# V of all head pairs computed ahead of the attention loop and kept in DRAM

## The chip, the core and the metric

The kernel runs on one core of one Trainium2 chip. The metric is the device time of one execution in microseconds (us). Engines: PE is TensorE (matrix products), DVE is VectorE, ACT is ScalarE, POOL is GpSimd, and SP issues all the DMAs spoken of here.

## The reference, cut to what matters

One layer of an encoder: neighbourhood attention, a layer norm, a squared-ReLU MLP with a gated embedding, a second layer norm. Only the attention's projections bear on the change.

```python
def neighborhood_attention(x, w_qkv, rpb, w_o):        # x (1, 1024, 1024), w_qkv (1024, 3072)
    qkv = (x @ w_qkv).reshape(bsz, rows, GRID_W, 3, NA_HEADS, HEAD_DIM)   # 16 rows, 64 wide, 16 heads of 64
    q = qkv[:, :, :, 0] * HEAD_DIM ** -0.5
    k = qkv[:, :, :, 1]
    v = qkv[:, :, :, 2]
    def row_block(r):                                  # 8 key rows, 16 key columns around each query
        s = jnp.einsum('bqhd,bakhd->bhqak', q_r, k_b, preferred_element_type=jnp.float32)
        s = jnp.where(col_in[:, None, :], s + bias, -jnp.inf)
        pr = jax.nn.softmax(s, axis=(-2, -1))
        return jnp.einsum('bhqak,bakhd->bqhd', pr.astype(v.dtype), v_b)
    ...
    return jnp.moveaxis(out, 0, 1).reshape(bsz, seq, D_MODEL) @ w_o
```

## The kernel before

**Numbers in two parts.** Each float32 operand of a projection is split into a high and a low part (ACT copies the high part, DVE or POOL subtracts for the low part), and a product is three passes: high by high, low by high, high by low. So one projection group (a bank of 128 x 512 outputs, 8 chunks of the inner dimension) is 24 products, `GROUP_MMS`.

**The first stage** (from L1386). x is loaded in eight column chunks, turned on PE, split, and kept as `act_T_hi` and `act_T_lo`. While the chunks come in, PE fills six banks: V, K and Q of head pair 0, two halves of the tokens each (`first_products`, L1265). V comes out with channels on the partitions, so DVE copies it to `v_T` (L1058), PE turns it by four 128 x 128 transposes per half (L1281), and ACT and DVE split the turned tile (L867, L1076) into `v_hi_lo`.

**The loop over head pairs** (`pairs_loop`: pairs 0 to 5 in a hardware loop, 6 and 7 apart). Each engine has its own queue with its own order, written out by steps s = 0 to 20 or 21. A pair has 16 score units (2 heads x 8 groups of 128 queries). On PE, step s holds a slice of the next pair's projections (`project`, L1227: 144 products over 20 steps, 7.2 each), the scores of unit s (L1310), the transposes of unit s-3's probabilities (L1289) and the products with V whose tiles are ready (L1333). Pair 7 has no next pair: PE then fills its steps with 96 embedding products (L1371) and the first output products.

The other queues run beside it. In step s of pairs 0 to 6:

- DVE: normalise unit s-2 (L1110, L1112), low part of turned tile s-4 (L1084), an output sum at s = 11, 13, 19, 21 (L1119), add the bias to the scores of unit s and take the negated maximum (L1103), then an evacuation of a projection group if one is due.
- ACT: high part of turned tile s-4 (L878), the half of an output sum (L894), an evacuation of a group (L841), exp of unit s (L887), which waits for the negated maximum of s, then a weight split if one is due (L833).
- POOL: the low halves of the weight splits (L778), and the two bias tables of the next pair (L785, L787).
- SP: weights of the pair after next, bias rows (16 DMAs per head), K's copies to the other half of the partitions (`k_twice`), the attention output.

In pair 7 the order on DVE is another: the bias add comes first in its step, ahead of normalise and low part.

`EVAC_STEP` gives the steps at which a group is evacuated: V at 3 and 6 (DVE) with its transposes at 4 and 7, K at 10 and 14, Q at 17 and 20. The splits of the weights on ACT are at steps 1, 9 and 18. These lines set the order on ACT and DVE for the pairs that the change touches:

```python
                    if PARTS <= s < UNITS + PARTS:
                        turned_tile(j, s - PARTS)
                    for h, b in out_evac_at(s):
                        out_sum(j, h, b)
...
                    if more and s < UNITS:
                        add_bias(j, s)
...
                    if more and s in EVAC_STEP[2:]:
                        evac(1 - par, j + 1, EVAC_STEP.index(s))
```

`add_bias(u)` waits for unit u's scores and for the exp of u-2; PE's scores of u wait for the bias add of u-2, its transposes of u for normalise of u, its V products of tile u for the low part of u. After pair 7 come the output projection, the layer norm and the MLP (from some 440 us on); the change leaves them alone.

Of the kernel before, what the change touches and what calls it, by code (L numbers as in the profile page):

```python
# [48 lines left out]
V_, K_, Q_ = range(3)  # L49
W_COLUMN = {V_: 2 * D, K_: D, Q_: 0}  # L50
# [73 lines left out]
def build_program(nc, x, p, w_qkv, rpb, w_o, ln1_g, ln1_b, w_ff1, w_ff2, ln2_g, ln2_b, w_gate, w_proj, mask, out):  # L124
    with ExitStack() as ctx:
# [15 lines left out]

        S.rpb_rows = nc.dram_tensor("rpb_rows", [GC, HEADS, DR, 3 * GC], F32).ap()
# [29 lines left out]
        with ExitStack() as first:  # L172

            S.w = [first.enter_context(nc.sbuf_tensor(f"w_qkv_{n}", [P, 2, KC, P], F32R)) for n in ("hi", "lo")]
            S.w_hi, S.w_lo = (first.enter_context(nc.semaphore(f"w_{n}_done")) for n in ("hi", "lo"))
            attention(nc, S, x, w_qkv, rpb, mask, w_o, p, w_proj, ln1_g, ln1_b, w_gate)
# [156 lines left out]
def attention(nc, S, x, w_qkv, rpb, mask, w_o, p, w_proj, ln_g, ln_b, w_gate):  # L333
# [5 lines left out]
    with ExitStack() as ctx:  # L339
# [7 lines left out]
        pair_places = [aligned(nc.sbuf_base)]  # L347
        q_st = sb("q_hi_lo", [P, 2, 2, T], F32R)

        k_st = []  # L350
        for n in ("hi", "lo"):
# [3 lines left out]
        v_T = sb("v_T", [P, T])  # L355
# [11 lines left out]
        spare = sb("spare", [P, 2])  # L367
        prob = sb("probabilities", [P, 4, NB])
# [17 lines left out]
        k_second_doubled = sem("rest_of_first_k_doubled")  # L386
        v_turned = sem("v_turned")
# [9 lines left out]
        ple_in = [sem(f"ple_raw_in{i}") for i in range(4)]  # L397
# [7 lines left out]
        early_in = [sem(f"attention_early_in{t}") for t in range(2)]  # L405
# [17 lines left out]
        x_first_in, w_first_in = S.raw_in[3], S.raw_in[V_]  # L423
        first_hi, first_lo = sem("first_w_hi_done"), sem("first_w_lo_done")

        first_q = sem("zeros_first_copy_and_first_q_done")
# [9 lines left out]
        x_places = [nc.alloc_sbuf_tensor_at(f"x_chunk{k}", [P, D], F32, offset=at)[:, :]  # L436
                    for k, at in enumerate(place + h * 4 * T for place in second_at for h in range(2))]
        x_places += [o_st[:, :], o_low[:, :, :].rearrange("p b q -> p (b q)")]
# [41 lines left out]
        def first_w(part, kind):  # L480

            if kind == Q_:
                both = v_cat[:, 1, :, :, :, :].rearrange("p g h a d -> p (g h a d)")
                return both[:, part * D:(part + 1) * D].rearrange("p (k n) -> p k n", k=KC)
            if kind == K_:
                return pT[part][:, :, :].rearrange("p s q -> p (s q)")[:, 0:D].rearrange("p (k n) -> p k n", k=KC)
            return S.w[part][:, V_, :, :]

        FIRST_BANK = {(V_, 0): 0, (V_, 1): 1, (K_, 0): 2, (K_, 1): 3, (Q_, 0): 4, (Q_, 1): 5}
        FIRST_ORDER = [(K_, 0), (V_, 0), (K_, 1), (V_, 1), (Q_, 0), (Q_, 1)]
        FIRST_KINDS = (K_, V_, Q_)

        FREED_ORDER = [(K_, 0), (V_, 0), (V_, 1), (K_, 1)]
# [3 lines left out]
        def first_count(kind, t):  # L499

            return FIRST_ORDER.index((kind, t)) + 1

        def freed_count(kind, t):

            return 4 + FREED_ORDER.index((kind, t)) + 1

# [4 lines left out]

        def x_highs(k, t):
            return 1 if k == 0 else 2 * k + t

        def first_raw(kind, k):
            return S.raw[:, 2 - kind, k * P:(k + 1) * P]
# [22 lines left out]
        def embed_place(u):  # L539
# [3 lines left out]
            return v_T[:, (u % 3) * HALF:(u % 3 + 1) * HALF]  # L543
# [15 lines left out]
        def pairs_loop(eng, body):  # L559

            with eng.Fori(0, PAIRS // 2 - 1) as it:
                for par in range(2):
                    body(2 * it + par, par, True, True)
            body(PAIRS - 2, 0, True, False)
            body(PAIRS - 1, 1, False, False)

        @block.sync
        def _(sp):
# [3 lines left out]
            def load_w(kind, offset, slot=None):  # L572
                sp.dma_start(S.raw[:, kind if slot is None else slot, :].rearrange("p (k n) -> p k n", k=KC),
# [14 lines left out]
            def k_half_twice(t):  # L588

                sp.wait_ge(proj_free, freed_count(K_, t))  # L590
                cols = slice(t * HALF, (t + 1) * HALF)
                for h in range(2):
                    own, other = slice(HEAD * h, HEAD * (h + 1)), slice(HEAD * (1 - h), HEAD * (2 - h))
                    done = k_second_doubled if t or h else k_doubled
                    for part in range(2):
                        sp.dma_start(k_st[part][other, 0, h, cols].bitcast(F32),
                                     k_st[part][own, 0, h, cols].bitcast(F32)).then_inc(done, 16)

            def k_twice(par, jn):

                written = value(6 * jn + (4 + 2))
# [8 lines left out]
            def credits():  # L610
                sp.sem_inc(out_stored, 16)
                sp.sem_inc(k_doubled, 32)
                for kind in (K_, Q_):
                    sp.sem_inc(S.raw_in[kind], 16)

            def load_first_w(k):
                src = bass.AP(w_qkv.tensor, w_qkv.offset + k * P * 3 * D, [[3 * D, P], [D, 3], [1, P]])
# [2222 lines left out]
```

## Time and profile before

| | us |
|---|---|
| median of 3 runs | 1225.35 |
| lowest, highest | 1225.02, 1225.45 |
| span of the profiled execution | 1223.4 |
| PE busy | 1213.5 (99%) |
| PE weight loads busy | 1020.1 (83%) |
| DVE busy | 883.5 (72%) |
| ACT busy | 593.6 (49%) |
| POOL busy | 103.9 (8%) |
| first stage | 0 to 48 |
| loop over pairs 0 to 6 | 48 to 397 |

The span runs from the first to the last instruction. A share of busy time is a mean over stages with different limits, so the stretches are read one by one. Matmuls are pipelined and their ends modelled: a product of 512 columns is shown as 0.39 us, while the next one starts 0.23 us after it. The start-to-start distance is the one that counts.

### The profile page before, as it was taken

What the parts mean: (1) busy time and instruction counts of PE and PEld (TensorE: products, weight loads), DVE (VectorE), ACT (ScalarE), POOL (GpSimd) and SP (SyncE); (2) the same over time, 40 slices, a digit from 0 to 9 for tenths busy, and PEclk for the clock granted to TensorE, in tenths of its full rate; (3) what the DMA queues carried; (4) which work ended last, traced back from release to release, by engine and by line L of the source; (5) the groups of instructions that cost most, each with busy time, mean ns of one, the idle gap of its engine ahead of it and who ended that gap; (6) DMA issues with size and microseconds to landing.
All of it is one profiled execution on the core that took longest, in us unless ns stands there. A gap on an engine that the chain in (4) does not pass through costs nothing.

```text
span 1223.4 us, 17911 instructions
## 1 busy us (share of the span) xinstructions
PE 1213.5 (99%) x5820; PEld 1020.1 (83%) x5820; DVE 883.5 (72%) x1744; ACT 593.6 (49%) x1144; POOL 103.9 (8%) x71
## 2 busy tenths in 40 slices
PE   9999999999999999999999999999999999999997
PEld 8888888888888888888888888888888888888886
DVE  3777677777777867769677777777764575588786
ACT  3555655655556843244444444444453433333671
POOL 0212222122123004200000000000000000000000
PEclk9999999999999999999999999999999999999999
DMA  8332223213233857683556566565579776768633
GB/s 219 83 76 71 58 72 89 55 55 75 55 107 84 274 158 233 209 286 118 192 207 240 177 221 218 184 239 178 220 239 379 280 274 223 258 238 309 192 104 103
DMA packets 162870, 215.61 MB, mean 176 GB/s; under 512 B 11504, under 2 KB 91504, under 8 KB 162416
## 3 DMA queue, kind: packets, MB, share of 16 engines
q1 hardware_dynamic: 162656, 214.59, 54.1%
q8 instruction: 39, 0.64, 0.2%
q14 instruction: 31, 0.25, 0.1%
q10 hardware_dynamic: 144, 0.13, 0.0%
HBM read 147.44 MB, written 58.90 MB: 169 GB/s over the span
## 4 chain that ended last, share of the span: by engine, by line
PE 98%; DMA 1%; DVE 0%; ACT 0%; issue 0%; DVEq 0%; SPq 0%; ACTq 0%
PE bank L2784 25%; PE bank L2752 25%; PE bank L1227 19%; PE bank L1378 7%; PE bank L2708 6%; PE bank L1333 4%; PE bank L1310 3%; PE bank L1289 3%; PE bank L1265 3%; PE bank L1371 1%; PE bank L1243 1%; PE bank L258 1%; PE bank L1281 1%; DMA ple_embedding<-bias_in 0%; DMA attention_T<-out_T 0%; DMA x_chunk<-in_x 0%
## 5 line engine op out<-in xcount | busy, mean ns | idle before, releaser
L887 ACT ACTIVATE probabilities<-negated_scores,negated_max 128x384 f32<-128x384 f32 (+1 forms) x128 | 75.7, 591 | 136.1 <-DVE negated_max L1103 135.7
L1227 PE MATMUL bank<-act_T_hi,w_qkv_hi 128*128 128x512 f32 x336 | 133.6, 398 | 0.0
L1227 PE MATMUL bank<-act_T_lo,w_qkv_hi 128*128 128x512 f32 x336 | 133.5, 397 | 0.0
L1227 PE MATMUL bank<-act_T_hi,w_qkv_lo 128*128 128x512 f32 x336 | 132.0, 393 | 0.0
L2752 PE MATMUL bank<-x_combination,weight_parts 128*128 128x512 f32 x504 | 118.5, 389 | 0.0
L1084 DVE TENSOR_TENSOR prob_T_lo<-bank,prob_T_hi 128x256 fp32r<-128x256 f32 (+2 forms) x160 | 69.1, 449 | 58.5 <-ACT prob_T_hi L878 56.8
L2752 PEld LDWEIGHTS bank<-x_combination,weight_parts 128*128 128x128 f32 x504 | 94.6, 188 | 19.6
L2752 PE MATMUL bank<-act_T_hi,weight_parts 128*128 128x512 f32 x240 | 77.3, 389 | 0.0
L2110 ACT ACTIVATE hidden_staging<-hidden_staging 128x512 f32<-128x512 f32 x48 | 30.4, 633 | 95.0 <-DVE hidden_staging L2450 95.0
L778 POOL TENSOR_TENSOR w_qkv_lo<-weight_raw,w_qkv_hi 128x1024 fp32r<-128x1024 f32 x21 | 50.3, 2396 | 294.5 <-ACT w_qkv_hi L833 294.5
L2784 PE MATMUL bank<-x_combination,hidden_parts_odd 128*128 128x512 f32 (+1 forms) x324 | 73.1, 381 | 0.0
L2784 PE MATMUL bank<-w_ff_parts,weight_parts_early 128*128 128x512 f32 x312 | 73.0, 389 | 0.0
L2784 PE MATMUL bank<-w_ff_parts,weight_parts 128*128 128x512 f32 x312 | 73.0, 389 | 0.0
L2784 PE MATMUL bank<-x_combination,weight_parts 128*128 128x512 f32 x312 | 73.0, 389 | 0.0
L1227 PEld LDWEIGHTS bank<-act_T_hi,w_qkv_lo 128*128 128x128 f32 x336 | 63.2, 188 | 10.7
L1227 PEld LDWEIGHTS bank<-act_T_hi,w_qkv_hi 128*128 128x128 f32 x336 | 63.2, 188 | 10.7
L1227 PEld LDWEIGHTS bank<-act_T_lo,w_qkv_hi 128*128 128x128 f32 x336 | 63.2, 188 | 9.7
L1112 DVE TENSOR_SCALAR probabilities<-probabilities,total_reciprocal 128x384 f32<-128x384 f32 (+1 forms) x128 | 66.6, 520 | 4.6
L2784 PEld LDWEIGHTS bank<-x_combination,hidden_parts_odd 128*128 128x128 f32 x324 | 59.3, 188 | 11.8
L2784 PEld LDWEIGHTS bank<-w_ff_parts,weight_parts 128*128 128x128 f32 x312 | 58.6, 188 | 12.2
L2784 PEld LDWEIGHTS bank<-x_combination,weight_parts 128*128 128x128 f32 x312 | 58.6, 188 | 12.2
L2784 PEld LDWEIGHTS bank<-w_ff_parts,weight_parts_early 128*128 128x128 f32 x312 | 58.6, 188 | 12.2
(263 smaller groups left out, 2806.6 us busy)
## 6 DMA issues: line engine op xcount, KB each, us to landing
hidden_combinations<-hidden_staging SPq DMA_DIRECT2D x112, 256.0 KB, 2.6
w_ff_in<-in_w_ff SPq DMA_DIRECT2D x27, 1024.0 KB, 8.1
weight_raw<-in_w_ff SPq DMA_DIRECT2D x25, 1024.0 KB, 5.7
weight_raw<-hidden_combinations SPq DMA_DIRECT2D x14, 1024.0 KB, 5.5
hidden_in<-hidden_combinations SPq DMA_DIRECT2D x14, 1024.0 KB, 5.6
weight_raw<-in_na_w_qkv SPq DMA_DIRECT2D x21, 512.0 KB, 4.4
bias_in<-rpb_rows SPq DMA_DIRECT2D x256, 6.0 KB
attention_T<-out_T SPq DMA_DIRECT2D x8, 512.0 KB, 3.2
```

The lines of the kernel that those rows point to most:

```text
L778: nc.gpsimd.tensor_tensor(w[1][:, slot, :, :], S.raw[:, raw, :].rearrange("p (k n) -> p k n", k=KC), w[0][:, slot, :, :].bitcast(F32), ALU ...
L887: nc.scalar.activation(prob[:, u % 4, 0:n], score[:, u % 2, 0:n], ACT.Exp, scale=-1.0, bias=nmax[:, u % 4:u % 4 + 1], accum_out=total[:, u ...
L1084: last = nc.vector.tensor_tensor(pT_part(pT[1], g, first, count), tile_ps[u % 2][:, at * P:(at + count) * P].rearrange("p (b q) -> p b q", ...
L1112: nc.vector.tensor_scalar(prob[:, u % 4, 0:n], prob[:, u % 4, 0:n], recip[:, u % 4:u % 4 + 1], None, ALU.mult).then_inc(prob_ready, 1)
L1227: mm = nc.tensor.matmul(proj_ps[gi % 2][:, :], w[wp][:, (par + kind) % 2, k, :], S.act[ap][:, k, t * HALF:(t + 1) * HALF], start=(i == 0), ...
L1265: mm = nc.tensor.matmul(S.ps[FIRST_BANK[kind, t]][:, :], first_w(wp, kind)[:, k, :], S.act[ap][:, k, t * HALF:(t + 1) * HALF], start=(k == ...
L1289: mm = nc.tensor.transpose(tile_ps[u % 2][:, i * P:(i + 1) * P], prob[:, u % 4, i * P:(i + 1) * P], S.ident[:, :])
L1333: mm = nc.tensor.matmul(out_ps[b][:, (mine[0] - 4 * b) * P:(mine[-1] + 1 - 4 * b) * P], v_cat[:, par, k, h, :, :].rearrange("p a d -> p (a ...
L1378: mm = nc.tensor.matmul(S.ps[2 * par + h][:, :], tile(ap, k), wo(wp, k)[:, h * HALF:(h + 1) * HALF], start=(k == 0 and n == 0), stop=(k == ...
L2708: mm = nc.tensor.matmul(bank, x, weights, start=(k == 0 and i == 0 and p in (1, 5, 6)), stop=(k == KH4 - 1 and i == 2), skip_group_check=p ...
L2752: mm = nc.tensor.matmul(bank, w1_part(wp, u, p)[:, k, :], x_part(ap, p, k), start=(k == 0 and n == 0 and p in (1, 5, 6)), stop=(k == KH4 - ...
L2784: mm = nc.tensor.matmul(bank, hid_part(ap, n, t)[:, k, :], weights(wp)[:, k, :], start=(start and k == 0 and i == 0), stop=(stop and k == ...
```

## The change

V of all eight pairs is computed first. x is now the stationary operand, 128 tokens at a time, and 512 columns of V's weights move, so V comes out with tokens on the partitions and needs no transpose. There are 16 tiles (2 halves of V's columns x 8 groups of tokens), 24 products each. Six of them take the place of the six groups of the first stage; ten follow, then the four groups of K and Q of pair 0, and then the loop. ACT and DVE split each tile into one of four places, SP stores it to `v_parts` in DRAM, and in the loop SP reads one pair's V (1 MB) a pair ahead. The loop's filling is K and Q only: 96 products over 20 steps, 4.8 each. `EVAC_STEP` becomes 5, 10 (K), 15, 20 (Q), and ACT's weight splits are at steps 1 (Q) and 12 (K). The order within a step of DVE and ACT stays. The core of the diff:

```diff
-FILL = 6 * GROUP_MMS
+PAIR_GROUPS = 4
+FILL = PAIR_GROUPS * GROUP_MMS
...
-EVAC_STEP = [(GROUP_MMS * (gi + 1) - 1) * FILL_STEPS // FILL + 1 for gi in range(6)]
-V_TURN_STEP = (4, 7)
+EVAC_STEP = [(GROUP_MMS * (gi + 1) - 1) * FILL_STEPS // FILL + 1 for gi in range(PAIR_GROUPS)]
...
+            def v_products(n, k, passes=(0, 1, 2)):
+
+                c, g = divmod(n, GROUPS)
+                for i in passes:
+                    wp, ap = PASSES[i]
+                    mm = nc.tensor.matmul(v_bank(n), S.act[ap][:, k, g * P:(g + 1) * P], w_v[wp][c][:, k, :],
+                                          start=(k == 0 and i == 0), stop=(k == KC - 1 and i == 2), skip_group_check=True)
+                if k == KC - 1:
+                    mm.then_inc(v_full, 1)
...
+            def v_tile(n):
+
+                if n >= GROUPS:
+                    pe.wait_ge(v_lo, n - GROUPS + 1)
+                for k in range(KC):
+                    if n == GROUPS:
+                        pe.wait_ge(w_lo, k + 1)
+                    v_products(n, k)
...
-                if (kind, t) in ((V_, 1), (Q_, 0)):
-                    turn_first_v(0 if kind == V_ else 1)
+            for n in range(FIRST_TILES, V_TILES):
+                v_tile(n)
+            pe.wait_ge(v_lo, GROUPS + 2)
+            project(0, 0, 0, FILL)
+            pe.wait_ge(v_lo, V_TILES)
...
+            def v_high(n):
+                act.wait_ge(v_full, n + 1)
+                if n >= V_PLACES:
+                    act.wait_ge(v_stored[n % V_PLACES], 16 * (n // V_PLACES))
+                nc.scalar.activation(v_place[n % V_PLACES][:, :, 0, :], v_bank(n).rearrange("p (e d) -> p e d", d=HEAD),
+                                     ACT.Copy).then_inc(v_hi, 1)
...
                     if s == 1:
-                        split((par + 1 + K_) % 2, K_, 16 * j + 32)
-                    if s == EVAC_STEP[1] + 2:
-                        act.wait_ge(proj_full, 6 * j + (6 + 2))
-                        split((par + 1 + Q_) % 2, Q_, 16 * j + 32)
-                    if loads and s == EVAC_STEP[3] + 4:
-                        act.wait_ge(proj_full, 6 * j + (6 + 4))
-                        split(par % 2, V_, 16 * j + 48)
+                        act.wait_ge(proj_full, PAIR_GROUPS * j + PAIR_GROUPS)
+                        split(Q_, j + 1)
+                    if loads and s == EVAC_STEP[1] + 2:
+                        act.wait_ge(proj_full, PAIR_GROUPS * j + (PAIR_GROUPS + 2))
+                        split(K_, j + 2)
...
-                    if more and s - 1 in V_TURN_STEP:
-                        turned_v(1 - par, j + 1, V_TURN_STEP.index(s - 1))
...
+            for n in range(GROUPS, V_TILES):
+                store_v(n)
+                if n == V_TILES - V_PLACES:
+                    for kind in (K_, Q_):
+                        sp.wait_ge(w_lo, split_count(kind, 0))
+                        load_w(kind, P)
+            for i in range(V_PLACES):
+                sp.wait_ge(v_stored[i], V_STORED)
+            load_v(0, 0)
+            k_twice(0, 0)
```

## Rows read from the trace of the kernel before

**Rows 1.** The page: the chain that ended last, by engine.

```profile
PE 98%; DMA 1%; DVE 0%; ACT 0%; issue 0%; DVEq 0%; SPq 0%; ACTq 0%
```

**Rows 2.** Busy time by stretch (us, PE, PEld, DVE, ACT, POOL, clock, DMA): pairs 0, 7.

```profile
49.50:99.05 49.55, 49.55 (x269) 42.85 (x268) 37.10 (x118) 28.20 (x69) 10.19 (x7) 1.00 0.26 63
...
396.30:436.00 39.70, 39.23 (x207) 32.54 (x206) 33.37 (x109) 34.24 (x80) 0.00 (x0) 1.00 0.77 262
```

**Rows 3.** Waits: who waited for whom, us in total, times, longest.

```profile
ACT probabilities L887 <- DVE negated_max L1103: 135.7, 105, 2.2
```

**Rows 4.** Order of time (start, us), DVE: bias adds of units 0, 4, 15.

```profile
100.10 0.42 DVE L1103 CUSTOM_DVE_ANT_0 negated_scores<-bank,bias_full 128x256 f32<-128x256 f32 x1
...
108.43 0.55 DVE L1103 CUSTOM_DVE_ANT_0 negated_scores<-bank,bias_inner 128x384 f32<-128x384 f32 x1
...
138.54 0.42 DVE L1103 CUSTOM_DVE_ANT_0 negated_scores<-bank,bias_full 128x256 f32<-128x256 f32 x1
...
149.65 0.42 DVE L1103 CUSTOM_DVE_ANT_0 negated_scores<-bank,bias_full 128x256 f32<-128x256 f32 x1
...
398.98 0.42 DVE L1103 CUSTOM_DVE_ANT_0 negated_scores<-bank,bias_full 128x256 f32<-128x256 f32 x1
```

**Rows 5.** Order of time, PE: scores of units 4 and 15 of pair 1.

```profile
107.23 0.34 PE L1310 MATMUL bank<-k_hi_twice,q_hi_lo 128*128 128x384 f32 x1
...
136.31 0.28 PE L1310 MATMUL bank<-k_hi_twice,q_hi_lo 128*128 128x256 f32 x1
```

**Rows 6.** Order of time, DVE, ACT, DVE: one turn of the ring.

```profile
111.24 0.55 DVE L1103 CUSTOM_DVE_ANT_0 negated_scores<-bank,bias_inner 128x384 f32<-128x384 f32 x1
...
111.84 0.62 ACT L887 ACTIVATE probabilities<-negated_scores,negated_max 128x384 f32<-128x384 f32 x1 [1.25 <-DVE negated_max L1103]
...
112.45 0.47 ACT L878 ACTIVATE prob_T_hi<-bank 128x384 fp32r<-128x384 f32 x1
...
112.96 0.56 DVE L1084 TENSOR_TENSOR prob_T_lo<-bank,prob_T_hi 128x384 fp32r<-128x384 f32 x1 [0.62 <-ACT prob_T_hi L878]
...
113.44 0.55 DVE L1103 CUSTOM_DVE_ANT_0 negated_scores<-bank,bias_inner 128x384 f32<-128x384 f32 x1
```

**Rows 7.** Order of time, PE: products around four V transposes.

```profile
44.04 0.39 PE L1265 MATMUL bank<-act_T_hi,w_qkv_lo 128*128 128x512 f32 x1
...
44.94 0.40 PE L1265 MATMUL bank<-act_T_lo,v_hi_lo 128*128 128x512 f32 x1
```

**Rows 8.** One line's instructions: V's low parts, ns least/median/most.

```profile
L1076 DVE TENSOR_TENSOR v_hi_lo<-bank,v_hi_lo x16: 681/692/692, 46.6 to 365.4; 128x512 fp32r<-128x512 f32 x16
```

**Rows 9.** The chain in order of time: output products, attention tile stationary.

```profile
470.42 10.90 PE bank L1378 x48
```

**Rows 10.** Order of time, PE and DVE: the first stage ends, pair 0 begins.

```profile
47.93 0.39 PE L1227 MATMUL bank<-act_T_hi,w_qkv_hi 128*128 128x512 f32 x1
...
49.69 1.39 DVE L1063 SCALAR_TENSOR_TENSOR q_hi_lo<-bank,q_hi_lo 64x512 fp32r<-64x512 f32 x2
...
51.12 0.42 DVE L1103 CUSTOM_DVE_ANT_0 negated_scores<-bank,bias_full 128x256 f32<-128x256 f32 x1
```

**Rows 11.** Order of time, SP's queue: issues of bias rows for two heads.

```profile
28.68 11.49 SPq L585 DMA_DIRECT2D bias_in<-rpb_rows  x32
```

**Rows 12.** Order of time, DVE: bias adds of units 10 and 11.

```profile
124.19 0.55 DVE L1103 CUSTOM_DVE_ANT_0 negated_scores<-bank,bias_inner 128x384 f32<-128x384 f32 x1
...
127.94 0.54 DVE L1103 CUSTOM_DVE_ANT_0 negated_scores<-bank,bias_inner 128x384 f32<-128x384 f32 x1
```

**Rows 13.** Order of time, ACT: a weight split at step 9.

```profile
122.25 1.04 ACT L833 ACTIVATE w_qkv_hi<-weight_raw 128x1024 fp32r<-128x1024 f32 x1
```

**Rows 14.** Order of time, POOL and DVE: a split, and two normalises.

```profile
103.80 2.39 POOL L778 TENSOR_TENSOR w_qkv_lo<-weight_raw,w_qkv_hi 128x1024 fp32r<-128x1024 f32 x1 [5.87 <-ACT w_qkv_hi L833]
...
104.08 2.32 DVE L1112 TENSOR_SCALAR probabilities<-probabilities,total_reciprocal 128x384 f32<-128x384 f32 x1
...
386.63 1.20 DVE L1112 TENSOR_SCALAR probabilities<-probabilities,total_reciprocal 128x384 f32<-128x384 f32 x1
```

More of the change, by code:

```diff
@@ L586, in load_bias @@
                       .then_inc(bias_loaded[h], 16)
[L588 to L597, printed above, removed]
             def k_twice(par, jn):
-                written = value(6 * jn + (4 + 2))
+                written = value(PAIR_GROUPS * jn + (2 + 2))
                 for h in range(2):
@@ L788, in build_bias, with body @@
                     .then_inc(bias_ready, 1)
-            split(1, V_, 4, 3)
+            for k in range(KC):
+                pool.wait_ge(w_hi, k + 1)
+                nc.gpsimd.tensor_tensor(w_v[1][1][:, k, :], v_raw(k), w_v[0][1][:, k, :].bitcast(F32),
+                                        ALU.subtract).then_inc(w_lo, 1)
+            for kind in (K_, Q_):
+                split(kind, 0)
+            pool.wait_ge(mask_loaded, 16)
             for h in range(2):
                 build_bias(h, 16 * ROWS)
-            def body(j, par, more, loads):
+            split(K_, 1)
+            def body(j, par, nth, more, loads):
                 if more:
-                    split((par + 1 + K_) % 2, K_, 3 * j + (3 + K_ + 1))
-                    split((par + 1 + Q_) % 2, Q_, 3 * j + (3 + Q_ + 1))
+                    split(Q_, j + 1)
                     pool.wait_ge(score_done, UNITS * j + (GROUPS + 2))
@@ L938, in _ @@
             act.sem_inc(exp_done, 2)
-            act.sem_inc(w_hi, 3)
             x_high(0, 0)
@@ L950, in _, with body @@
                 x_high(k, 1)
-                if k == 5:
-                    split(1, V_, 32, 3)
-            first_evac(K_, 0)
-            first_evac(K_, 1)
-            turned_v(0, 0, 0)
-            first_evac(Q_, 0)
-            turned_v(0, 0, 1)
-            first_evac(Q_, 1)
-            def body(j, par, more, loads):
+            for n in range(V_TILES):
+                v_high(n)
+                if n < KC // 2:
+                    second_split(2 * n)
+                    second_split(2 * n + 1)
+                if n == GROUPS:
+                    for kind in (K_, Q_):
+                        split(kind, 0)
+            for gi in range(PAIR_GROUPS):
+                evac(0, 0, gi)
+                if gi == 1:
+                    split(K_, 1)
+            for i in range(V_PLACES):
+                act.wait_ge(v_stored[i], V_STORED)
+            def body(j, par, nth, more, loads):
                 for s in range(STEPS + 1):
@@ L1150, in wo_low, with body @@
                 nc.vector.tensor_tensor(wo(1, n), S.raw[:, n % 4, :], wo(0, n).bitcast(F32), ALU.subtract).then_inc(wo_lo, 1)
-            def body(j, par, more, loads):
+            def body(j, par, nth, more, loads):
                 for s in range(STEPS + 1):
@@ L1413, in _ @@
             for k in range(1, KC - TAIL):
-                for n, (t, kind) in enumerate((t, kind) for t in range(2) for kind in FIRST_KINDS):
+                for n in range(FIRST_TILES):
                     if n == 2:
@@ L1420, in _, with body @@
                             turn_x(k + 2, half)
[L1421 to L1422 removed]
+                    first_products(n, k)
+            for n in range(FIRST_TILES):
                 for k in range(KC - TAIL, KC):
[L1424 to L1428 removed]
+                    first_products(n, k)
+            for n in range(FIRST_TILES, V_TILES):
[3 more added lines that the diff above has]
+            pe.wait_ge(v_lo, V_TILES)
+            def body(j, par, nth, more, loads):
                 for s in range(STEPS):
```

327 lines of the change are left out of this document (144 added, 183 removed).

## The prediction

> A(u) is the start of DVE's bias add (L1103) of score unit u, u = 0 to 15 in each pair; "loop body" is the work of one pair.
>
> **What bounds the kernel now.** I read the page's chain of work first. PE is 98% of the chain that ended last [rows 1], so any product taken from PE looks like a gain. Next, busy time by stretch: in one loop body of 49.55 us PE is full, DVE has 37.10, ACT 28.20, POOL 10.19 [rows 2]. DVE seems to have 12 us to spare. The list of waits says otherwise: ACT sat idle 135.7 us, 105 times, before its exponential, always for DVE's negated maximum [rows 3]. Then the order of time on DVE: A(0) of pair 1 is at 100.10, A(4) at 108.43, A(15) at 138.54, A(0) of pair 2 at 149.65 [rows 4]. On PE the scores of units 4 and 15 start at 107.23 and 136.31 [rows 5], 29.1 us apart, while the bias adds are 30.1 apart: over these eleven steps DVE falls behind PE, by 1.2 us at first and 2.2 at the end. The scores are already there, so something other than PE paces the adds.
>
> It is a ring of two queues written in a fixed order. In step s, ACT does the high part of tile s-4, any evacuation, then exp(s); DVE does the low part of tile s-4, any output sum, then the bias add of s. So exp(s-1) -> high part -> low part -> add(s) -> exp(s) is serial. In rows: add at 111.24, exp 111.84, high 112.45, low 112.96, next add 113.44 [rows 6]: 2.20 us, with no PE in it. PE hides this only because its own mean full step is as long: 29.1/11 = 2.64.
>
> **The change part by part.** *Removed from PE:* the V transposes. Four of them stand between the product that starts at 44.04 and the second one behind it at 44.94 [rows 7]: 0.90, where two gaps of 0.23 would be 0.46. That is 0.44 per half, 16 halves, 7.0 us. Removed from DVE are 16 copies of V's bank. Its 16 low parts of 0.69 [rows 8] and ACT's high parts move: the new tiles need 16 of each, now beside the V products.
>
> *Moved on PE:* nothing else disappears. V is 16 tiles x 24 = 384 products in place of 8 x 48. With x stationary they should cost the same: 48 products with the attention tile stationary took 10.90, or 0.227 each [rows 9]; K and Q products start 0.23 apart [rows 7, 10]. Of these, the six first tiles replace the six groups of the first stage (144 products); ten more (240) and pair 0's K and Q in full (96) stand ahead of the first scores. The first stage ended at 47.93 [rows 10]. So pair 0's Q is complete at 47.93 - 0.9 + 240 x 0.227 + 96 x 0.228 = 123.4. Its last ACT and DVE evacuation take 1.2 + 1.4 (DVE's is the row of 49.69 [rows 10]; ACT's pairs of copies are a little shorter), so A(0) of pair 0 is at 126.1 instead of 51.12 [rows 10]: **+75.0**. I cost at nothing: the tile evacuations (0.6 + 0.69 per tile of 24 x 0.227 = 5.4 us); POOL's eight low halves (half of one of the splits below each, 9.6 in all, needed only for tile 8, some 10 us after the last of their loads); SP's 16 stores, the pair-by-pair reads of 1 MB (each is asked for a whole body ahead), and the two bias loads of SP, whose 32 issues take 11.5 us [rows 11] and now stand between stores 7 and 8. If that cover fails, V waits: see the rivals.
>
> *The bodies.* Each of seven loses 48 products (11.0 us) and two transpose halves (0.9): PE's share falls from 49.5 to 37.6, a full step from 2.64 to 2.64 - 2.4 x 0.23 - 0.88/11 = 2.0. The ring is longer than that, so now it paces. Read step by step from pair 1, less what goes (DVE's low V part, 0.69, in steps 5 and 8, and the wait for PE at 9):
> - Plain steps: 2.20, or 1.96 to 2.33 by the tile's width. Seven of them in A(4) to A(15), at 4, 6, 7, 8, 9, 11, 13, and 14 since Q now goes at 15: eight, together 17.5.
> - Step 5 has K's first evacuation: as at step 10 of before, add 0.62, two ops 1.42, normalise and low part 1.1: 3.17.
> - Step 10 has K's second and an output sum: 124.19 to 127.94 [rows 12], 3.75.
> - Step 12 has the output sum (2.95 in pair 1) and now the K split, which holds up the high part by 0.95 (the next high part starts that much after the split of 122.25, 1.04 long [rows 13]): 3.9.
> Sum 28.3. It was 30.1; only 1.8 us come back where PE has lost 7. Add 0.3: POOL's bias build no longer waits behind the Q split, so it starts on A(7); in pair 6 such a start met the normalise of 386.63 and made it 1.20 instead of 0.42 [rows 14]. II = 28.6.
> - I, A(0) to A(4), was 8.33. PE's steps of 4.8 products allow 5.5. But the split at step 1 stays and with it the block of a normalise by POOL (2.39 from 103.80, DVE's 2.32 from 104.08 [rows 14]). With A(2) at 2.0 and A(3) at 3.5, POOL runs from 3.0 to 5.4, then normalise, low part: A(4) at 6.3.
> - III, A(15) to the next A(0), was 11.1. By PE alone it would be 11.1 - 12 x 0.23 = 8.4. DVE's own work there is the Q evacuation (now at 15) 1.9 with the add, two normalises 1.1, four low parts 2.0, two sums 1.4, the last evacuation 1.4: 7.8. Neither can run alone: the last normalise waits for the Q evacuation (to 2.2), PE's transposes for that (3.1), its last products end at 6.6; from there ACT's evacuation 1.2, DVE's 1.4 and an output sum 0.7: 10.0.
> One body 6.3 + 28.6 + 10.0 = **44.9** against 49.55 in pair 1 and a mean of (398.98 - 51.12)/7 = 49.69 for all seven [rows 4, 10]; the difference is pair 6, which also carries the embedding's copies and transposes. With half its cover gone I give it 47.2.
>
> **Sum.** A(0) of pair 7 at 126.1 + 6 x 44.9 + 47.2 = 442.7, instead of 398.98 [rows 4]: +43.7. From there on nothing in the order changes. The span 1223.4 is 2 us under the median of 1225.35; on the median I forecast **1269.0**.
>
> **The rivals.**
> *(a) The ring keeps up* (the 2.2 us are slack taken because it was there, and adds and exponentials close up when PE presses). For it: DVE and ACT have idle time, and pair 7, whose queues put the add ahead of the low part, takes 96 embedding products and 16 units in about 39.7 us with PE at 39.23 [rows 2]. Against it: the diff leaves the old order in the other pairs, and each link in rows 6 starts when the one before ends. It decides if a full step can be done in 2.0 us. Price: -7.0, 1218.4. Faster than before. Chance 0.05.
> *(b) Only II is the ring's;* I and III follow PE at 5.5 and 8.6, a body is 42.4, pair 6 44.5: 425.0, +26, **1251**. The walk through I and III is my least sure step. 0.15.
> *(c) The V stage is not hidden:* stores or the second half of the weights come late behind SP's 11.5 us of bias issues, PE waits once or twice, about one such queue, +10: **1279**. 0.10.
> *(d) PE's clock falls.* PE now rests for 7.3 of 44.9 us per body. The granted clock is 1.00 in every stretch read, pair 7 with its short rests included [rows 2], and none shows a lower one. If the 512-column cadence doubled at 1.2 GHz, PE's 37.6 us would be 75 and a body 30 longer; one body in seven so gives 1299, all 1479. 0.04. The Trainium skill, "TensorE: Matmul & The Clock Gate", section "What's actually happening", has this rule: an idle array falls back to half clock. It speaks against leaving PE to wait; these rests are spread, under a microsecond per step, so I let the row decide.
> *(e) The forecast:* 0.66.
>
> The range takes in (b), (c) and the spread of (e), where a body may be 44 to 46: **1248 to 1284**, with about 1 in 10 outside. 0.2% is about what a measurement of this kernel can tell from no change. Faster 0.05 (all of (a)), same 0.01, slower 0.94.
>
> **What would show it.** Right: first scores of pair 0 near 124; A(0) to A(0) near 45; A(4) to A(15) near 28.5, with PE idle or waiting for DVE in L1289, L1310 or L1333, some 7 us a body; ACT's exponential still waiting for L1103; no L1281; the pair 7 stretch unchanged. Wrong: a body near 38 to 40 with DVE above 90% (a); PE gaps between 47 and 123 (c); a granted clock below 1.00 (d); V products not at 0.227.

## The result, and the profile after

The kernel after takes 1276.98 us (median of 4 runs, 1275.14 to 1277.98), against 1225.2 us of the kernel before timed beside it: ratio 1.0418, 95% interval 1.0406 to 1.0431. It is slower by 51.8 us; 43.7 was forecast, and 1277.0 lies inside the range of 1248 to 1284. The profiled execution has a span of 1275.4 us.

The chain that ended last, by engine (kernel after, the page). PE had 98% of it before [rows 1]:

```profile
PE 75%; issue 9%; ACT 8%; DVE 6%; DVEq 0%; ACTq 0%; DMA 0%
```

Busy time by stretch (kernel after; us, then PE, PEld, DVE, ACT, POOL busy, granted clock, DMA share, GB/s): the later V products and the body of pair 0. The second answers to [rows 2]:

```profile
38.30:102.25 63.95, 63.95 (x284) 52.93 (x283) 11.67 (x17) 15.36 (x27) 17.71 (x14) 1.00 0.55 170
126.72:171.29 44.57, 39.10 (x212) 32.51 (x211) 33.28 (x112) 26.16 (x66) 7.93 (x6) 1.00 0.31 79
```

From 38.3 us to the end of the V stage PE is never idle. In a body it is now idle for 5.5 us of 44.57, where it was idle for none of 49.55. Pair 7 is unchanged: from its A(0) to its A(15) it takes 33.30 us before and 33.29 after, and from its A(0) to the end of the profile both take 824.4.

The list of waits (kernel after; who waited for whom, us, times, longest), which answers to [rows 3]:

```profile
ACT probabilities L908 <- DVE negated_max L1109: 115.9, 84, 7.3
...
DVE prob_T_lo L1090 <- ACT prob_T_hi L899: 61.8, 80, 1.6
...
PE bank L1284 <- DVE prob_T_lo L1090: 34.8, 44, 1.2
...
PEld bank L1284 <- DVE probabilities L1118: 23.9, 22, 1.6
```

ACT waits for DVE and DVE for ACT, and PE now waits for DVE: 34.8 us for the low part, where the kernel before has 0.2. That is the ring of the forecast, no longer hidden by fill products.

Order of time on DVE (kernel after; start, us). The first line is A(0) of pair 0, the next three are A(0), A(4) and A(15) of pair 1, then the end of pair 1 and A(0) of pair 2, last A(0) of pair 7. They answer to [rows 4, 10]:

```profile
126.72 0.43 DVE L1109 CUSTOM_DVE_ANT_0 negated_scores<-bank,bias_full 128x256 f32<-128x256 f32 x1
...
171.29 0.42 DVE L1109 CUSTOM_DVE_ANT_0 negated_scores<-bank,bias_full 128x256 f32<-128x256 f32 x1
...
176.87 0.55 DVE L1109 CUSTOM_DVE_ANT_0 negated_scores<-bank,bias_inner 128x384 f32<-128x384 f32 x1
...
205.07 0.42 DVE L1109 CUSTOM_DVE_ANT_0 negated_scores<-bank,bias_full 128x256 f32<-128x256 f32 x1
...
215.13 0.69 DVE L1125 TENSOR_TENSOR out_T<-bank,out_low_part 64x512 f32<-64x512 f32 x1
217.58 0.06 DVE L1108 MEMSET spare<- 128x1 f32 x1 [1.76 <-issue]
220.56 0.42 DVE L1109 CUSTOM_DVE_ANT_0 negated_scores<-bank,bias_full 128x256 f32<-128x256 f32 x1 [2.92 <-issue]
...
450.96 0.42 DVE L1109 CUSTOM_DVE_ANT_0 negated_scores<-bank,bias_full 128x256 f32<-128x256 f32 x1
```

A(0) of pair 0 comes at 126.72, 75.6 us later than before. The plain pairs (0 and 5) take 44.57 and 44.55 us. Two pairs do not: from A(15) to the next A(0) pair 1 takes 15.49 us (205.07 to 220.56) and pair 3 16.10, where pairs 0, 2, 4 and 5 take 10.8. In that stretch of pair 1 DVE stands still twice, for 1.76 and 2.92 us (2.04 and 3.25 in that of pair 3), and the profile names nothing that it waits for ("issue"). The pairs run two by two in a hardware loop, and pairs 1 and 3 are those after which it jumps back. The forecast knew nothing of this. Behind the stall PE's clock drops (kernel after, by stretch, then order of time on PE):

```profile
217.00:221.00 4.00, 0.19 (x1) 0.00 (x0) 0.50 (x5) 0.00 (x0) 0.00 (x0) 0.98 0.99 336
221.00:225.00 4.00, 3.95 (x13) 3.39 (x14) 2.31 (x12) 2.75 (x7) 1.75 (x1) 0.59 0.56 178
225.00:229.00 4.00, 4.00 (x23) 3.44 (x22) 2.74 (x13) 2.71 (x8) 0.63 (x1) 1.00 0.46 129
```

```profile
221.05 0.69 PE L1301 MATMUL bank<-k_hi_twice,q_hi_lo 128*128 128x384 f32 x1 [3.86 <-DVE negated_max L1109]
...
221.85 0.63 PE L1223 MATMUL bank<-act_T_hi,w_qkv_lo 128*128 128x512 f32 x1
```

After 3.86 us without work most of the next 4 us run at the 1.2 GHz level (a granted clock of 0.59 in the mean), and a product lasts 0.63 us in place of 0.39. The Trainium skill, "TensorE: Matmul & The Clock Gate", section "What's actually happening", says that an idle array falls back to half clock; this row agrees.

### The profile page after: what moved, and what is told of

Read it like the earlier page. It is cut to its first block, busy times and chain, and to the rows that moved or that the text cites. A ratio compares the mean times of both kernels' runs of the same rounds, so it can differ in the third digit from the quotient of the medians.

```text
span 1275.4 us, 17657 instructions
## 1 busy us (share of the span) xinstructions
PE 1221.4 (96%) x5756; PEld 1014.7 (80%) x5756; DVE 865.8 (68%) x1712; ACT 592.5 (46%) x1131; POOL 102.7 (8%) x74
## 4 chain that ended last, share of the span: by engine, by line
PE 75%; issue 9%; ACT 8%; DVE 6%; DVEq 0%; ACTq 0%; DMA 0%
PE bank L2775 24%; PE bank L2743 24%; PE bank L1369 7%; PE bank L1253 7%; PE bank L2699 6%; PE bank L1223 3%; ACT prob_T_hi L899 2%; ACT probabilities L908 2%; DVE prob_T_lo L1090 2%; PE bank L1324 1%; PE bank L1284 1%; ACT k_hi_twice L864 1%; PE bank L1362 1%; ACT q_hi_lo L864 1%; DVE k_lo_twice L1081 1%
## 5 line engine op out<-in xcount | busy, mean ns | idle before, releaser
L1223 PE MATMUL bank<-act_T_lo,w_qkv_hi 128*128 128x512 f32 x256 | 102.7, 401 | 0.0
L1223 PE MATMUL bank<-act_T_hi,w_qkv_hi 128*128 128x512 f32 x256 | 102.5, 400 | 0.0
L1223 PE MATMUL bank<-act_T_hi,w_qkv_lo 128*128 128x512 f32 x256 | 101.9, 398 | 0.0
L1284 PE MATMUL bank<-identity,probabilities 128*128 128x128 f32 x352 | 61.1, 278 | 35.9 <-DVE prob_T_lo L1090 34.8
L1284 PEld LDWEIGHTS bank<-identity,probabilities 128*128 128x128 f32 x352 | 41.5, 140 | 57.0 <-issue 28.8
L899 ACT ACTIVATE prob_T_hi<-bank 128x256 fp32r<-128x256 f32 (+2 forms) x160 | 59.6, 398 | 27.2 <-PE bank L1324 26.2
L1118 DVE TENSOR_SCALAR probabilities<-probabilities,total_reciprocal 128x384 f32<-128x384 f32 (+1 forms) x128 | 60.0, 468 | 4.5
L2240 DVE TENSOR_TENSOR weight_parts<-weight_raw,weight_parts 128x512 fp32r<-128x512 f32 x51 | 35.1, 690 | 34.4 <-ACT weight_parts L2010 34.4
```

Of the source, the lines that this page charges most:

```text
L899: last = nc.scalar.activation(pT_part(pT[0], g, first, count), tile_ps[u % 2][:, at * P:(at + count) * P].rearrange("p (b q) -> p b q", b= ...
L1118: nc.vector.tensor_scalar(prob[:, u % 4, 0:n], prob[:, u % 4, 0:n], recip[:, u % 4:u % 4 + 1], None, ALU.mult).then_inc(prob_ready, 1)
L1223: mm = nc.tensor.matmul(proj_ps[gi % 2][:, :], w[wp][:, kind, k, :], S.act[ap][:, k, t * HALF:(t + 1) * HALF], start=(i == 0), stop=(i == ...
L1284: mm = nc.tensor.transpose(tile_ps[u % 2][:, i * P:(i + 1) * P], prob[:, u % 4, i * P:(i + 1) * P], S.ident[:, :])
L2240: nc.vector.tensor_tensor(w1_part(1, u, p), w1_source(u, p), w1_part(0, u, p).bitcast(F32), ALU.subtract).then_inc(s_lo, 1)
```

## Experiments: the two stalls at the loop's branch

Does DVE wait there for its own instructions? The pages list the packets of an instruction queue, q14, of 8192 bytes each, first for the kernel before, then for the one after:

```profile
q14 instruction: 31, 0.25, 0.1%
...
q14 instruction: 41, 0.34, 0.1%
```

Does the place of DVE's code decide? The edit puts cheap instructions ahead of everything on DVE.

```diff
+            for i in range(16):
+                nc.vector.memset(score[:, 1, i:i + 1], 0.0)
             nc.vector.memset(score[:, 0, 0:P], 0.0).then_inc(first_step, 1)
```

**a_pad16** (kernel after, 16 clears).

> The kernel after, with 16 clears of one column of an unused score buffer put ahead of everything on VectorE, where it waits for its first input; nothing else is changed. They only move VectorE's loop by 16 instructions. If the two stalls of 4.7 and 5.3 us at the loop's back branch (the stretch from the bias add of step 15 to the next pair's first is 15.49 and 16.10 us after pairs 1 and 3, and 10.79 us after pairs 0, 2, 4 and 5) come of where VectorE's loop lies against the blocks in which instructions are loaded, they vanish: 10.8 us after pairs 1 and 3 too, no instruction loads in the loop's second and third turn, and 1277.0 - 9.9 = about 1267 us. If they come of something in the pair's work itself (a late transfer, a wait on PE), nothing changes: 1277 us, 15.5 and 16.1 us again.

Measured 1264.93 us, ratio 1.0316 (1.0299 to 1.0333), 12.0 us less than the kernel after. The stretch behind A(15) is 10.78 to 10.80 us in all of pairs 0 to 5, and 31 packets are left on q14. Sixteen useless instructions gained 0.9%. This is the clean kernel on which the further experiments build; its body (by stretch) is

```profile
170.88:215.41 44.53, 39.23 (x213) 32.79 (x213) 33.11 (x112) 26.13 (x66) 7.93 (x6) 1.00 0.32 88
```

**b_pad16** (kernel before, the same clears).

> The kernel before, with the same 16 clears ahead of everything on VectorE. If the place of VectorE's loop decides, this kernel's loop, which has 27 instructions more than that of the kernel after, now crosses one block more: instruction loads show in each turn, and after pairs 1 and 3 the stretch from the bias add of step 15 to the next first one goes from 11.1 us to 15 to 16 us. Each stall costs what it is long, since PE waits too at the pair's end: 1225.4 + 5 to 10 = 1230 to 1235 us. If place has nothing to do with it: 1225.4 us, 11.1 us.

Measured 1224.79 us, ratio 0.9991 (0.9982 to 1.0001), 32 packets, 11.1 us at all pairs' ends: nothing changed, where I had forecast 1230 to 1235. My guess that the longer loop would now cross one block more was wrong in its size, and it gave the bound for a sharper one, counted in blocks of 128.

**b_pad64 and a_pad96** (the same edit with 64 clears before, 96 after).

> The kernel before with 64 clears of one column each ahead of everything on VectorE. VectorE's loop has 471 instructions in the kernel before and 444 in the one after, and 112 and 103 stand ahead of it. 16 clears took the loads away from the kernel after and brought none to the kernel before. If VectorE's instructions are loaded in blocks of 8192 bytes (the size of the packets on that queue; 128 instructions of 64 bytes) and four such blocks stay loaded, then a loop of 471 fits only if it begins within the first 41 instructions of a block: it does so as it stands (4 to 12 behind a block's start, by what 16 clears did in the two kernels) and with 16 clears (20 to 28), and no longer with 64 (68 to 76). Then loads show in each turn, the stretch from the bias add of step 15 to the next first one grows from 11.1 us to 15 to 16 us after pairs 1 and 3, and the time to 1230 to 1237 us. If the loop's place in such blocks isn't the cause, it stays at 1225 us.

> The kernel after with 96 clears in place of 16. By the same blocks of 128 instructions of which four stay loaded, a loop of 444 fits if it begins within the first 68 of a block: with 16 clears it begins at 11 to 19, with 96 at 91 to 99, and it crosses into a fifth. Then the stalls of 4.7 and 5.3 us are back: 1265 + 10 = 1275 us. If the 16 clears helped by something else (a later start of VectorE's first work, say), more of them don't bring the stalls back: 1265 us.

Both stall where the count says: 42 packets each, in b_pad64 12.92 and 12.89 us behind A(15) of pairs 1 and 3 in place of 11.08, in a_pad96 12.55 and 12.57 in place of 10.8. The stall is one gap of 1.76 us instead of two (order of time, DVE, a_pad96):

```profile
215.43 0.69 DVE L1125 TENSOR_TENSOR out_T<-bank,out_low_part 64x512 f32<-64x512 f32 x1
217.87 0.06 DVE L1108 MEMSET spare<- 128x1 f32 x1 [1.76 <-issue]
217.91 0.42 DVE L1109 CUSTOM_DVE_ANT_0 negated_scores<-bank,bias_full 128x256 f32<-128x256 f32 x1
```

The size was forecast too large (5 us). The times of the packets in the traces explain one gap against two. In the kernel after one packet comes at 215.44, behind the jump, and DVE goes on at 217.27. It starts only four instructions of the loop, stands still again until the next packet, of 218.46, is in, and goes on at 220.56. In a_pad96 the two packets come at 215.74 and 218.73, and DVE works through the second: with 96 instructions put ahead of it the loop has some 36 to go to its block's end. a_pad96 takes 1270.18 us, ratio 1.0365 (1.0347 to 1.0382), 5.3 above a_pad16. Its A(0) of pair 7 comes 4.4 us later.

b_pad64 takes 1226.12 us, ratio 1.0006 (0.9997 to 1.0016), where I had forecast 1230 to 1237: two stalls of 1.8 us that cost nothing. By stretch (b_pad64), across the first:

```profile
149.00:153.00 4.00, 4.00 (x21) 3.37 (x20) 2.13 (x8) 0.15 (x2) 0.00 (x0) 1.00 0.10 18
```

PE is full while DVE stands still: it does the next pair's fill ahead, and A(0) to A(4) of that pair takes 5.85 us in place of 8.3 (the eleven steps behind it 30.76 in place of 30.1). The kernel before has a cover of 7.2 fill products a step for such a stall; with 4.8, and bound by DVE and ACT anyway, the kernel after gets nothing back.

How large is what stays loaded? The two expectations above count 444 and 471 instructions in the loop and four blocks. The traces show another count. From one jump to the next they list 314 instructions of DVE in the kernel after, 330 in the one before and 346 in a_pad_ring (below). In the kernels that stall, five packets come in each later turn, at the same places in both turns within two instructions: two at the jump and three behind 24, 140 and 259 instructions in the kernel after, 37, 166 and 296 in a_pad96, 69, 196 and 321 in b_pad64. They lie 116 to 130 apart, which is a block of 128 of the listed instructions. Count the blocks from the end of one four instructions into the loop of the kernel after (the loop of the kernel before begins five later), and all seven kernels fit one rule: where the loop lies in three blocks, the later turns load nothing (no packet from 213 to 400 us in a_pad16); where it reaches into a fourth, each loads five, the four blocks and one ahead. That three blocks and the one ahead are what stays loaded is inferred from these seven places. The count of the expectations would allow nearly the same places, but not packets so far apart.

The Trainium skill, "Runtime: NRT & Kernel Launch", section "Instruction fetch mechanics", states the mechanism: a taken branch whose target is not in the loaded window has to fetch it first. The gaps at the branch agree. It gives 32 KiB of instructions in blocks of 16 KiB; here four blocks of 8192 bytes, loaded one by one, fit the runs.

## Experiments: what sets a body

**b_fill96** takes products from the kernel before and nothing else; in `project`:

```diff
+                    if i % 3 == 1:
+                        continue
                     mm = nc.tensor.matmul(proj_ps[gi % 2][:, :], w[wp][:, (par + kind) % 2, k, :],
```

> The kernel before with every third product of the fill left out (the middle pass of the three, of V, K and Q alike), so that each pair's fill has 96 products instead of 144, spread as before; all evacuations, transposes and splits stay, and the output is not the reference's. 48 x 0.227 us x 7 = 76 us less work on PE. By the ring (ScalarE's exponential, its high part, VectorE's low part, the bias add, 2.2 us per step) a pair gives back only what lies above the ring: steps 0 to 4 about 2.0 us, steps 4 to 15 about 1.5 us, the rest 1 us, so a pair of 49.55 us becomes 45 to 46 us and the time 1225.4 - 7 x 4 = 1197 us (1190 to 1205). If PE alone set the pair (the rival in which the ring keeps up), it becomes 49.55 - 10.9 = 38.7 us and the time 1149 us.

Measured 1196.72 us, ratio 0.9762 (0.9745 to 0.9778). 76 us of PE's work gave back 29. A body (by stretch):

```profile
97.04:142.27 45.23, 40.76 (x222) 33.46 (x221) 34.90 (x116) 28.03 (x69) 10.28 (x7) 1.00 0.30 75
```

A(0) to A(4) is 6.1, A(4) to A(15) 29.45, then 9.70: of the 4.3 us that the pair gives back 2.2 come from steps 0 to 4, 0.65 from the eleven steps in which the ring paces, 1.4 from the end. The rival in which the ring keeps up (1149 by this edit) has fallen.

**a_pad_fill48** goes on in the same direction, from a_pad16:

```diff
+                    if drop and i % 2 == 0:
+                        continue
```

> The kernel with the 16 clears, with every second product of K and Q left out in pairs 1 to 7 (the output is not the reference's): the fill has 48 products a pair instead of 96, spread as before. That is 10.9 us less work on PE a pair, 76 us in all. By the ring, with 144 to 96 products a pair gave 5 us, and the next 48 give little: steps 4 to 15 stay at 28.2 us (up to 0.5 less), steps 0 to 4 at 5.5 us, only the stretch behind step 15, in which evacuation and PE take turns, gives 0.5 to 1.5 us; a pair of 44.55 becomes 42.5 to 44, the time 1265 - 7 x 0.5 to 2 = 1251 to 1261 us. If PE's products still set the pair, it becomes 34 to 36 us and the time 1190 to 1205 us.

Measured 1261.67 us, ratio 1.0291 (1.0274 to 1.0308), 3.3 us less than a_pad16. A body (by stretch):

```profile
213.81:257.58 43.77, 29.84 (x164) 23.20 (x164) 33.47 (x113) 26.12 (x66) 7.90 (x6) 1.00 0.31 88
```

A(4) to A(15) stays at 28.18 us with PE idle a third of the time. I had forecast 0.5 to 2 us a body; it was 0.8, and the pair with the last copies grew, so the time is just above the bound. With b_fill96 this gives the price list of fill products, per body: 144 products 49.55 us, 96 products 45.23 (44.55 without V's other work), 48 products 43.77. The first 48 are worth 4.3 us of PE's 10.9, the next 0.8. (By the ratios alone a_pad_fill48 and a_pad16 are barely apart; A(0) of pair 7, at 435.61 against 439.20 us, says the same as their times.) PE's clock fell six times in the loop of this run, to 0.57 in the mean from 287 to 295 us, and the pair in which that lies still took 43.78 us (the next, with a fall from 332 us on, 44.06): there PE's time hardly counts.

**a_pad_ring** lengthens the ring and leaves PE alone; in `add_bias` of a_pad16:

```diff
+                if more:
+                    nc.vector.memset(embed_out_tile[:, (u % 2) * 256:(u % 2) * 256 + 256], 0.0)
                 nc.vector.memset(spare[:, u % 2:u % 2 + 1], 0.0)
```

> The kernel with the 16 clears, and in pairs 0 to 6 one more clear, of 256 columns of a buffer unused until the last pair, ahead of each bias add on VectorE. VectorE is idle a quarter of a pair (33.2 of 44.55 us busy), PE's work is unchanged. A clear of 128 columns took 0.17 us, so this one takes 0.2 to 0.3. By the ring each step grows by the whole of it: steps 4 to 15 by 11 x 0.2 to 0.3 = 2.2 to 3.3 us, the pair by 12 to 16 of them, 2.5 to 4.8 us, and the time by 18 to 34 us, to 1283 to 1299 us. If PE or the depth of the buffers sets the pair, VectorE's idle time takes it up: under 0.5 us a pair, 1265 to 1268 us.

Measured 1289.09 us, ratio 1.0520 (1.0502 to 1.0537), 24.2 us more than a_pad16. The clear and the body (by line, and by stretch):

```profile
L1109 DVE MEMSET embedding_place<- 128x256 f32 x112 | 30.5, 272 | 1.3
...
222.02:270.04 48.02, 40.00 (x214) 32.40 (x213) 37.24 (x130) 26.25 (x66) 7.92 (x6) 1.00 0.29 81
```

Of 11 x 0.272 = 2.99 us, A(4) to A(15) takes 2.72; of 16 x 0.272 = 4.35 the body takes 3.5, though DVE had 11.4 us of idle time in it. Idle time in a ring isn't slack.

**a_pad_order** tries to cut the ring with the order of pair 7. On DVE (and on ACT likewise for the exponential):

```diff
-                    if not more and s < UNITS:
+                    if s < UNITS:
                         add_bias(j, s)
                     if NORMAL <= s < UNITS + NORMAL:
                         normalise(j, s - NORMAL)
...
-                    if more and s < UNITS:
-                        add_bias(j, s)
```

> The kernel with the 16 clears, and in pairs 0 to 6 the order that pair 7 has already: VectorE puts the bias add of a step ahead of the normalising and the low part, ScalarE the exponential ahead of the evacuations. This cuts the ring: the exponential of a step needs no low part of the same step. If the ring holds the pair at 44.6 us, it falls toward PE's 39.1 us of work, at 40 to 42 us, and the time to 1267 - 7 x 2.6 to 4.5 = 1236 to 1249 us. If the pair is held by something else (the chain from scores to weighed values through all steps, or the number of score buffers), it stays at 44 to 45 us and the time at 1267 us.

Measured 1277.12 us, ratio 1.0409 (1.0392 to 1.0427), 12.2 us more than a_pad16: a miss, with the sign wrong. A body takes 46.0 to 47.0 us. Order of time on PE (a_pad_order), in place of small rests:

```profile
232.65 0.52 PE L1282 MATMUL bank<-identity,probabilities 128*128 128x128 f32 x3 [1.83 <-DVE prob_T_lo L1088]
```

The bias add now stands ahead of the low part. PE's next transposes need that low part to free their bank, and behind them in PE's queue wait the fill and the next scores. Was it a second ring, through PE with the fill inside? From A(4) to A(15) a body takes 28.2 to 29.3 us, hardly more than the 28.2 of a_pad16; most of the loss stands behind A(15), 12.55 against 10.78, of which about 1 (an estimate from a normalise of 0.42 and a low part of 0.56) is only the add's earlier place in its step. What makes the rest of the end longer was not followed up.

**a_pad_order_f48** has both edits:

> The kernel a_pad_order with every second product of K and Q left out in pairs 1 to 7 (the output is not the reference's). a_pad_order was slower than a_pad16 (pairs of 46 to 47 us against 44.55), though its exponential waits for no low part of its step. Reason now held: its bias add runs ahead of the low part of the same step, the next transposes on PE wait for that low part (1.9 us each), and with them the fill and the scores of the next step, so that the ring now goes through PE and takes the step's 4.8 fill products (1.1 us) with it. Then 2.4 products less a step shorten each ring step by 0.5 us: steps 4 to 15 from 28.3 to 29.3 down to 22 to 25 us, the pair to 38 to 42 us and the time to 1277 - 7 x 5 to 8 = 1221 to 1242 us. If VectorE's and ScalarE's order alone still sets it, as in a_pad16, it changes as little as there (1264.9 to 1261.7): 1270 to 1275 us.

Measured 1252.73 us, ratio 1.0219 (1.0201 to 1.0236). The same 48 products a body that were worth 3.3 us in a_pad16 are worth 24.4 here, so in this order PE's fill does lie in the path that sets the body. But the forecast of 1221 to 1242 was too good. A(4) to A(15) is 24.8 to 26.2 us, and the steps behind K's evacuation still take 3.96 us with few products: order of time on PE (a_pad_order_f48) across one:

```profile
232.54 0.34 PE L1301 MATMUL bank<-k_lo_twice,q_hi_lo 128*128 128x384 f32 x1
234.97 0.52 PE L1284 MATMUL bank<-identity,probabilities 128*128 128x128 f32 x3 [2.10 <-DVE prob_T_lo L1088]
```

DVE's evacuation (1.39), its add, normalise and low part stand between PE and its bank. I had sized the ring by the plain steps. Each order of these queues has its own ring; none tried is free.

## Experiments: the stage that was added, and the end of a pair

**a_pad_v_two** takes a third of V's products from a_pad16; in `v_products`:

```diff
                 for i in passes:
+                    if i == 1:
+                        continue
```

> The kernel with the 16 clears and the middle of the three passes of the V products left out (the output is not the reference's); in the stretch from 38.3 to 102.25 us that is a third of its 282 products, 94 x 0.2268 = 21.3 us. Nothing else of the stage is taken away: the splits of the second half of V's weights, the evacuation of 16 tiles and their stores stay. If the stage is PE's alone, each product costs its whole 0.2268 us: the first bias add comes at 126.3 - 21.3 = 105 us and the time is 1264.9 - 21.3 = 1244 us (1242 to 1246; a little less is gained if loads set the first 38 us and nothing is gained there). If ScalarE, VectorE or the loads are close behind PE, the stage gives back less, down to 10 us: 1255 us.

Measured 1238.3 us, ratio 1.0101 (1.0084 to 1.0118), 26.6 us less. A(0) of pair 0 (order of time, DVE, a_pad_v_two), at 126.33 in a_pad16:

```profile
99.08 0.42 DVE L1109 CUSTOM_DVE_ANT_0 negated_scores<-bank,bias_full 128x256 f32<-128x256 f32 x1
```

That is less than the 1242 to 1246 expected, since I had counted only the 94 products after 38.3 us. In all 128 are gone, 29.0 us at 0.2268, and 27.25 came back: here a product costs nearly all of its time, the early ones under the first loads too.

**a_pad_fs18 and a_pad_fs17** ask why the end of a pair took 10.8 us and not 10.0. They end the fill earlier:

```diff
-FILL_STEPS = STEPS - 1
+FILL_STEPS = 18
```

> The kernel with the 16 clears and the 96 products of the fill spread over 18 steps of a pair instead of 20 (5.3 a step instead of 4.8; the four groups end in steps 4, 8, 13 and 17, Q's last evacuation lies in step 18 instead of 20). In a_pad16 the stretch from the bias add of step 15 to the next pair's first, 10.8 us, ends with Q's evacuation on VectorE (1.39 us) between the two output sums, and 10 fill products (2.2 us) lie on PE behind the last transposes. Reason held: pairs are set by the ring and by this late evacuation, not by the sum of PE's work; then the stretch shrinks to 9.0 to 9.6 us, steps 4 to 15 stay at 28.2 us, steps 0 to 4 grow by at most 0.3, the pair is 43.2 to 43.8 us and the time 1265 - 7 x 0.8 to 1.4 = 1255 to 1260 us. If PE's sum of work counts, it doesn't matter where the products lie: 44.5 us, 1265 us.

> The same with the 96 products over 17 steps (5.6 a step, Q's last evacuation in step 17). If the late evacuation counts, no more is gained than over 18 steps, since the output sums then end the pair alone: 1253 to 1260 us; steps 4 to 15 may grow where an evacuation now meets another slow step, by up to 0.5 us a pair.

Measured 1288.48 us, ratio 1.0515 (1.0494 to 1.0537), and 1269.45 us, ratio 1.0357 (1.0337 to 1.0376): both misses. The end did shrink in the pairs in which the clock held, to 9.2 and 7.9 us, so Q's late evacuation did stand there. But A(0) to A(4) grew from 5.58 to 8.5 and 7.1, and A(4) to A(15) from 28.2 to 29.2 and 29.1. PE's scores of unit 0 started 1.7 us ahead of A(0) in a_pad16 and start 0.4 ahead of it here: the fill that used to be done while DVE ended the pair now stands ahead of the next scores. In a_pad_fs18 the weight split on POOL comes on top: it begins 0.08 us ahead of a normalise on DVE, which then takes 2.54 us, against 1.43 in a_pad16 (order of time, DVE, a_pad_fs18):

```profile
174.02 2.54 DVE L1118 TENSOR_SCALAR probabilities<-probabilities,total_reciprocal 128x384 f32<-128x384 f32 x1
```

At best a body was 44.1 us (a_pad_fs17, pairs 1 to 3) against 44.55. What pairs 0 to 3 gained there pairs 4 to 6 lost again: A(0) of pair 7 comes at 439.22 us, in a_pad16 at 439.20. And PE, left without fill at the end, lost its clock. By stretch, a_pad_fs18 across the end of pair 1:

```profile
205.00:212.00 7.00, 5.78 (x34) 4.44 (x32) 6.00 (x19) 3.59 (x12) 1.59 (x2) 1.00 0.02 3
212.00:215.00 3.00, 0.89 (x3) 0.57 (x4) 2.39 (x5) 1.75 (x4) 0.00 (x0) 0.88 0.09 14
215.00:218.36 3.36, 3.36 (x12) 2.91 (x13) 1.08 (x3) 0.59 (x1) 0.00 (x0) 0.60 0.09 13
```

In a_pad_fs17 the same at the end of pair 4 (by stretch; 0.56):

```profile
335.00:341.00 6.00, 4.46 (x27) 3.52 (x28) 5.18 (x19) 3.93 (x12) 1.58 (x2) 1.00 0.01 1
341.00:347.20 6.20, 5.15 (x19) 4.47 (x18) 3.12 (x7) 1.75 (x4) 0.00 (x0) 0.56 0.08 15
```

Why pair 7, whose code is unchanged, also grew by 2.6 us in both stays open.

## Why the prediction was right, step by step

**The sign and the mechanism** held. PE's 98% of the chain was no promise of a gain: 336 products, 48 of V in each of seven bodies, went from a stretch that ACT and DVE pace as well to one that is PE's alone. b_fill96, a_pad_fill48 and a_pad_ring show the first half, a_pad_v_two the second.

**A(0) of pair 0**: forecast 126.1, measured 126.72. The later V products ran at 282 in 63.95 us, 0.2268 each, as taken from the output products; the gaps for tile evacuations, POOL's halves, stores and SP's bias issues were covered as claimed (PE 63.95 of 63.95). Rival (c) fell.

**The body**: forecast 44.9, measured 44.57. Its parts were less exact than the sum. A(0) to A(4) was 6.3 by forecast and is 5.58. A(1) follows A(0) after 0.36 us, since PE has both scores ready, so A(2) and A(3) come 0.3 earlier than forecast; POOL's split runs from 2.7 to 5.1 us behind A(0) (3.0 to 5.4 by forecast), but the normalise under it has begun long before and ends 0.2 behind it, so that of DVE's block of 2.32 us in the kernel before 1.41 are left. A(4) to A(15) was 28.6 and is 28.2: steps 5, 10 and 12, forecast at 3.17, 3.75 and 3.9, took 3.17, 3.64 and 3.89, and the 0.3 for POOL's bias build was not needed. The end was 10.0 and is 10.8: I had overlooked that PE's transposes of the last tile but one wait for the low part two tiles back, 0.6 to 0.8 us, so that Q's last products end at 7.4 behind A(15) and not at 6.6. Rival (b), which gave PE's own time to the first and last part, was right for the first (5.5) and wrong for the end (8.6); its body of 42.4 also took 28.3 for the middle where the forecast took 28.6.

**Pair 6**: forecast 47.2, measured 45.64. The fear for its cover was 1.6 us too large.

**The sum**: A(0) of pair 7 was forecast at 442.7 and came at 450.96. The difference of 8.3 is 0.6 from A(0) of pair 0; -0.33 for each of six bodies, -2.0; -1.6 from pair 6; and +11.2 from the stalls at the loop's branch (4.7 and 5.3, and 0.6 in each of the two pairs behind). With the stalls away the kernel takes 1264.9, 4 us under the forecast; with them it is 8 us above. So the closeness of the number owes something to luck: no step of the sum had the instruction loads, and the list of waits could not have shown them, since the kernel before has none in its loop.

**Rival (d)**, the clock: it fell, but for 3 to 4 us at a time and only behind the stalls. A plain body, whose rests on PE are at most 1.2 us each with fill between, keeps a clock of 1.00. The row that I let decide held for the plain bodies; the stalls, which no row before could show, brought the fall in.

## What to carry to other kernels

An engine with 98% of the chain may have a second limit right under it: before moving its work, walk one step through the queues of the others, and ask what the stretch takes when the work is gone and what it costs where it goes. Work that an in-order queue does while it waits is paid once in the old place and again in full in the new one, and it also covers stalls and holds up the clock. When a hardware loop's body changes length, compare the ends of its turns with each other before explaining anything by the change itself.

## What the runs showed of the hardware

- DVE's loop loads its instructions again in each turn when it reaches into a fourth block of 128 listed instructions (the kernel after, a_pad96, b_pad64), and not when it lies in three (the other four). The loads show as one gap of 1.8 us at the jump, or as two, of 1.76 and 2.92 or 2.04 and 3.25; in the kernel after they cost 12 us, and 16 clears of one column remove them.
- The same stall of 1.8 us costs the kernel before nothing (1226.1 against 1225.2 us), because PE works ahead through it.
- PE fell to the 1.2 GHz level without one long rest: in a_pad_fs18 it was busy for 0.89 us of 3.00, its longest rest there was 1.76 us, and the next 3.36 us had a granted clock of 0.60.
